# First late sum directly behind the last gated values, second late rows' norm ahead of the last half sums

## What is computed

```python
x = x + hier_moe(rmsnorm(x, p['norm2_g']), p)      # top-1 of 4 groups, then top-2 of its 4 experts
y = rmsnorm(x, final_norm_g)

def rmsnorm(x, g):
    y = xf * lax.rsqrt(jnp.mean(xf * xf, axis=-1, keepdims=True) + RMS_EPS)
    return y * g

h = silu(u @ expert_w_gate) * (u @ expert_w_up)    # EXPERT_FF = 256, 16 experts
h = h * combine                                    # the routing weight of the token
return h @ expert_w_down                           # summed over the experts
```

## Time and profile before

| | us |
|---|---|
| median of 3 runs | 812.12 |
| lowest and highest | 810.83, 812.77 |
| profiled execution, its time | 812.26 |
| profiled execution, span from first to last instruction | 810.7 |
| PE, DVE, ACT, POOL busy | 778.4, 431.0, 212.0, 38.8 |

### The profile page before, as it was taken

How to read it: one execution, slowest core, us unless ns; L and a number is a source line. 1 busy time by engine, 2 the same in 40 slices (tenths; PEclk the granted TensorE clock), 3 DMA queues, 4 the chain that set the end, 5 groups by cost and what they waited for, 6 DMA issues and landing times.

```text
span 810.7 us, 19968 instructions
## 1 busy us (share of the span) xinstructions
PE 778.4 (96%) x8538; PEld 536.7 (66%) x8538; DVE 431.0 (53%) x854; ACT 212.0 (26%) x498; POOL 38.8 (5%) x49
## 2 busy tenths in 40 slices
PE   7999999999999999999999999999999879999993
PEld 5877777787767877777777877767788633333331
DVE  4965667588768565657666555346204431101125
ACT  4122222254523312211212232220022411111144
POOL 0000000000000000000000000000000011222121
PEclk9999999999999999999999999999999889999998
DMA  9541432422212101201230112064935679999973
GB/s 332 184 160 56 130 109 76 161 105 74 82 53 80 53 28 56 68 15 49 73 124 29 32 52 80 3 231 199 358 132 198 238 303 405 392 402 385 370 232 151
DMA packets 36534, 126.91 MB, mean 157 GB/s; under 512 B 5752, under 2 KB 16024, under 8 KB 31584
## 3 DMA queue, kind: packets, MB, share of 16 engines
q1 hardware_dynamic: 32560, 115.78, 38.0%
q0 software_dynamic: 3888, 9.87, 4.3%
HBM read 106.31 MB, written 18.68 MB: 154 GB/s over the span
## 4 chain that ended last, share of the span: by engine, by line
PE 89%; DMA 4%; DVE 3%; ACT 2%; issue 2%; SPq 0%; POOL 0%; POOLq 0%; DVEq 0%; ACTq 0%
PE psum L1370 23%; PE psum L1351 12%; PE psum L1703 10%; PE psum L2594 9%; PE psum L2626 4%; PE psum L1328 4%; PE psum L1315 2%; PE psum L1303 2%; PE psum L1571 2%; DVE arena L2050 2%; PE psum L1659 1%; PE psum L1584 1%; PE psum L2574 1%; PE psum L1468 1%; PE psum L1480 1%
## 5 line engine op out<-in xcount | busy, mean ns | idle before, releaser
L2050 DVE TENSOR_TENSOR arena<-arena 128x268 f32<-128x268 f32 (+10 forms) x322 | 175.2, 544 | 49.2 <-ACT arena L1802 29.8
L1370 PE MATMUL psum<-arena 128*128 128x268 f32 x784 | 189.5, 393 | 0.0
L1370 PEld LDWEIGHTS psum<-arena 128*128 128x128 f32 x784 | 145.1, 189 | 37.8 <-issue 11.6
L1802 ACT ACTIVATE arena<-psum 128x268 f32<-128x268 f32 (+7 forms) x215 | 85.5, 405 | 276.9 <-PE psum L1370 146.6
L2050 DVE TENSOR_TENSOR arena<-psum,arena 128x256 f32<-128x256 f32 (+5 forms) x170 | 71.7, 425 | 80.9 <-PE psum L1584 21.8
L1351 PE MATMUL psum<-arena 128*128 128x268 f32 x392 | 105.0, 402 | 0.0
L1703 PE MATMUL psum<-arena 128*128 128x268 f32 x384 | 91.0, 391 | 1.6 <-DVE arena L2050 1.2
L2594 PE MATMUL psum<-arena 128*32 128x512 f32 (+1 forms) x640 | 85.8, 598 | 0.5 <-DVE arena L2747 0.3
L1351 PEld LDWEIGHTS psum<-arena 128*128 128x128 f32 x392 | 69.7, 189 | 20.4 <-issue 6.3
L1703 PEld LDWEIGHTS psum<-arena 128*128 128x128 f32 x384 | 71.1, 189 | 17.7 <-issue 3.3
L2747 DVE TENSOR_TENSOR arena<-psum,arena 128x256 f32<-128x256 f32 (+2 forms) x38 | 24.3, 663 | 104.2 <-ACT arena L2661 90.8
(11 more groups left out here) (207 smaller groups left out, 695.0 us busy)
## 6 DMA issues: line engine op xcount, KB each, us to landing
arena<-in_w_gu SPq DMA_DIRECT2D x16, 2048.0 KB, 20.3
arena<-in_w_in SPq DMA_DIRECT2D x45, 512.0 KB, 4.4
arena<-in_w_dn SPq DMA_DIRECT2D x16, 1024.0 KB, 19.0
arena<-in_w_out SPq DMA_DIRECT2D x2, 2048.0 KB, 14.1
arena<-arena SPq DMA_DIRECT2D x5, 536.0 KB, 5.6
arena<-in_x SPq DMA_DIRECT2D x8, 268.0 KB, 5.5
arena<-arena SPq DMA_DIRECT2D x16, 134.0 KB, 4.4
arena<-in_x SPq DMA_DIRECT2D x1, 2144.0 KB, 14.5
```

The costliest lines, as they stand in the source:

```text
L1370: last = mm(ps, w[:, k, :], x[:, k, :], start=(k == 0 and i in (0, 1, 3)), stop=(k == KD // 2 - 1), skip_group_check=i not in (0, 1, 3))
L1802: run(nc.scalar.activation(out, in_, fn, **kw), s)
L2050: run(v.tensor_tensor(out, a, b, op), s)
```

## The change

`summed(0)` with its wait for the gathers stands ahead of `normed(2)` instead of behind it, directly behind `hidden(11)`. `normed(TT + 1)` stands ahead of the two half sums instead of behind them and the epsilon step. Nothing is added or removed, and the order of the norms among themselves, and so of the counts of `z_y`, is the same.

```diff
                     normed(0)
                     normed(1)
                     hidden(NPASS - 1)
-                    normed(2)
                     at_least(dve, z_in, 16 * LATE, 16 * LATE)
                     summed(0)
-                    normed(3)
-                    normed(4)
+                    for t in range(2, TT):
+                        normed(t)
                     summed(1)
                     normed(TT)
+                    normed(TT + 1)
                     for q in range(2):
                         x = late[:, LATE - 1, 512 * q:512 * q + 512]
                         at_least(dve, q_dn if q else q_dh, NPASS if q else 1, NPASS if q else 1)
...
                     at_least(dve, z_hs, 1, 1)
                     v.tensor_scalar(fs[:, TT + LATE:TT + LATE + 1], fs[:, TT + LATE:TT + LATE + 1], EPS, None,
                                     ALU.add).then_inc(z_hb, 1)
-                    for t in range(TT + 1, TT + LATE):
-                        normed(t)
+                    normed(TT + 2)
```

## The result

The changed kernel took 813.79 us in the median of 14 runs, the kernel before 811.81 us beside it (14 runs). One of the changed kernel's runs took 4392.63 us, in a slow state that nothing here explains, and does not enter the ratio. The ratio is 1.0021, with a 95% interval of 1.0012 to 1.0030: slower by about 1.7 us (the medians as they stand differ by 1.98), where +0.7 us was forecast. The time is inside the stated range (811.4 to 814.1), but it came out at the edge of 0.2%, not well within it. The profiled execution took 812.94 us, 0.7 us above that of before, with a span of 811.4 us. So the two profiled executions show the forecast step, and the ratio of all runs shows one that is 1.0 us larger. Why both are true is the subject of the experiments.

The account below looks back on a forecast made before the run. The end was taken to hang on the closing chain through DVE and ACT's roots, not on PE. Third scatter +0.82 us less 0.09 gives +0.73; 812.12 + 0.7 = 812.8 us, range 811.4 to 814.1.

Parts of the forecast that it names:

- The second part: On DVE, norm of TT + 1 ahead of the half sums: third scatter +0.82 us, less G.
- PE's wait: PE's 1.01 us wait for the first late sum before its last product: would go, but the end does not hang on it.
- G: Gain on DVE from the first late sum ahead of block 2's norm: 0.09 us, bounds -1.40 to 0.96.
- R: When DVE can take block 2's root (its ACT start plus 0.33 us); the forecast used 792.49.
- Z: When DVE can take the first late sum, after the third gather lands; the forecast used about 792.4.
- the likeliest case: Gathers landing near 792.24: +0.3 to +1.1 us; range with the spread of medians 812.0 to 813.7 us.
- The prediction's own sign: Wrong if the third scatter's start moves over 1 us from 806.8, or anything ahead of 789 us moves.
- The gathers are late: Rival: first late sum heads DVE's remaining work, late gathers uncovered; up to 2.22 us cost, 814.3; chance 0.13 (over 0.5 us).
- The gathers are early: Rival: first late sum runs inside DVE's idle time after the gated values; -0.14 us, 812.0; chance 0.12.
- PE's wait was what counted: Rival: half sums wait for PE's last product, so ending its wait brings up to 1.0 us, 811.1; chance 0.02.

Follow-up runs that it names:

- six executions: One profiled execution each: kernel before (two), changed kernel (two), each of the two moves by itself; Z - R was -1.2 to +2.5 us.
- first part alone: Against the kernel before, only the first late sum moved ahead of block 2's norm; ratio 1.0009 (1.0000 to 1.0017).
- the profile with fewer loads: Only the first late sum moved, with SP's loads of blocks 3 and 4 held until the last gate and up product; ratio 0.9989 against the kernel before.

## Why the prediction came out as it did

**The second part was right in mechanism and size.** Forecast +0.82 us, measured 0.81 to 0.82 us in three profiles (9.05, 9.06 and 9.06 us less 8.24), and 1.0013 in the ratio, whose interval (1.0000 to 1.0025) holds it. The new idle time ahead of the last reciprocal was forecast at 0.9 us and is 0.83; the wait ahead of the norm of TT + 1 at 0.24 and is 0.15 (with 0.09 us of an ordinary gap). The third scatter started at 806.79; 806.8 was forecast.

**PE's wait was rightly discounted.** It went from 1.01 to 0.44 us. That it was not zero is a small miss: pass 10's product ended about 1 us earlier in this execution, so PE stood at the sum sooner.

**The step that was mis-sized is G**, "792.49 - 792.40 = 0.09 us". Both terms were taken from one execution as if the order fixed them. R hangs on two row loads, ACT's squares and two table loads, Z on three gathers; neither waits for the other. In the six executions R lay between 790.75 and 793.77, 792.2 in the mean, and Z between 792.3 and 793.7, 792.9 in the mean. In the changed kernel's own profile the second term came out as forecast (792.37) and the first did not: G is 791.54 - 792.37 = -0.83 us. From the ratios G is -0.7 us (first part alone) to -0.9 us (1.7 less 0.8), and the sum becomes 1.5 to 1.7 us; 1.7 and 1.8 us were measured. Of the likeliest case neither the step, +0.3 to +1.1 us, nor the range of medians, 812.0 to 813.7 us, came true.

**The agreement of the two profiled executions is luck.** The forecast of +0.7 us for the profiled execution came true (812.94 against 812.26) because the execution of before that was profiled had a late root: with the changed kernel's R of 791.54 it would have been 0.95 us shorter. The prediction's own sign caught this. It was to be wrong if something ahead of 789 us moved, and something did: the last gated values start at 788.38 instead of 789.33, with code that the change doesn't touch. ACT's first square of a row block shows where it comes from, before and after: block 0 was loaded 0.95 us sooner.

```profile
784.67 1.06 ACT L2689 ACTIVATE arena<-arena 128x1024 f32<-128x1024 f32 x1 [4.12 <-DMA arena<-x_rows]
```

```profile
783.72 1.06 ACT L2689 ACTIVATE arena<-arena 128x1024 f32<-128x1024 f32 x1 [3.56 <-DMA arena<-x_rows]
```

**The rivals.** "The gathers are late" had the right mechanism, a sum at the head of the queue with nothing over a late landing, but I put it down to a landing that varies, with a chance of 0.13, and left the root out: an early root loses its head start in the new order. Against the forecast's 792.49 and 792.40, the six executions have the root 0.3 us earlier in the mean and the landing 0.5 us later; in the changed kernel's own profile it was the root alone. "The gathers are early" happened in one execution of six, and there by a late root, not an early landing (in the profile with fewer loads by an early landing, 791.03). The fit by which a gather would land in an estimated 3.2 us (the Trainium skill, page "DMA: Bandwidth & Descriptors", section "Anatomy of one DMA — SWDGE (gpsimd) path") was met by none of them here: the shortest landing of one of these gathers in any profile was 5.9 us. "PE's wait was what counted" is refuted by the first part alone: PE's wait fell to 0.56 us and its last product ended at 798.07, DVE took the half sums only at 800.93, and the stretch up to the third scatter kept its 8.24 us.

**What was not foreseen in place.** The second scatter was forecast near 802.9 and started at 803.21, held by the first, whose issue took 1.61 us. It did not matter, as POOL had 2.6 us of idle time behind it.

## What to carry to other kernels

When two waits end at nearly the same time, the order of the two is a bet on which comes last; take several profiled executions and compare the two moments in each, since one execution gives the sign by chance. Work that is ready for certain belongs ahead of a wait on a loaded DMA queue, as a cover: here one norm of 1.40 us ahead of the sum was worth some 0.7 us by the ratio (0 to 1.4 us by its interval). The same rule spoke against the second part from the start: a short independent step put ahead of the longest remaining chain delays that chain by its full length, and it leaves the chain's own gap uncovered. Here the half sums came 1.6 us later behind the second late sum, DVE idled 0.83 us, and the end moved by 0.81 us.

## What the hardware showed that was not expected

GpSimd's issue of a scatter took 0.96 to 1.00 us when VectorE was idle or took one operand from PSUM (and 1.00 us with a multiplication of two SBUF operands under its last 0.16 us only the earlier trace rows), 1.38 us when a multiplication of two SBUF operands overlapped its first 0.54 us (803.46 + 0.20 + 1.29 - 804.41), and 1.61 us in the changed kernel, where such a multiplication (800.74 to 802.03) overlapped its first 0.74 us. The added 0.4 and 0.6 us are each some 0.1 to 0.2 us less than the overlap. Every profile has the same: 1.38 to 1.39 us in the eleven without the second part, 1.60 to 1.61 us in the three with it. No run took the overlap away on purpose. The Trainium skill, page "SBUF — State Buffer", section "Who interferes with whom", says that a VectorE instruction with two SBUF inputs contends with a GpSimd instruction that reads SBUF; the profiles here agree, with these times.

The time of a gather of 128 rows from issue to landing went from 5.9 us (table loads away and two row loads held) to 11.2 us (the old order, with the same two loads held), so what was held back doesn't alone set it. Issued 1.9 us later the third gather landed only about 1 us later.
